# A fused two-model block on one core: output weights converted outside the attention heads, scaled blocks of four norms written to PSUM

## The reference, cut to what matters

```python
a = rmsnorm(h, norm_mix_pre[i])
m = mla_mixer(a, ...) if i % N_MIXERS == 0 else pool_mixer(a, ...)
h = h + rmsnorm(m, norm_mix_post[i])
f = conv_ffn(rmsnorm(h, norm_ffn_pre[i]), ...)
h = h + rmsnorm(f, norm_ffn_post[i])
```

## Time and profile before

| | |
|---|---|
| median of three runs | 1041.41 us (1040.64 to 1042.99) |
| profiled execution | 1039.17 us, span 1037.4 us |
| PE busy | 953.3 us, 92% of the span |
| DVE / ACT / POOL busy | 747.4 / 503.1 / 355.8 us |
| mean granted TensorE clock | 0.933 of full speed |

### The profile page before, as it was taken

How to read it: one execution, slowest core, us unless ns; L and a number is a source line. 1 busy time by engine, 2 the same in 40 slices (tenths; PEclk the granted TensorE clock), 3 DMA queues, 4 the chain that set the end, 5 groups by cost and what they waited for, 6 DMA issues and landing times.

```text
span 1037.4 us, 20011 instructions
## 1 busy us (share of the span) xinstructions
PE 953.3 (92%) x7208; PEld 905.5 (87%) x7208; DVE 747.4 (72%) x1304; ACT 503.1 (48%) x831; POOL 355.8 (34%) x226
## 2 busy tenths in 40 slices
PE   6788999799999899679999989799998999999995
PEld 6786668699999899669999989798998999999995
DVE  7658652689999722658999963477968788786566
ACT  5464333555555443455556643345345545454432
POOL 4421003422222454342222246532125433335543
PEclk9898558799999999789999999989999999999998
DMA  7223001334444445113445545415323555565531
GB/s 268 103 82 122 1 0 42 122 123 162 162 162 177 168 173 206 41 41 123 162 167 178 198 164 202 169 67 196 121 82 133 174 191 202 170 225 175 200 122 41
DMA packets 20848, 145.64 MB, mean 140 GB/s; under 512 B 2480, under 2 KB 4032, under 8 KB 5440
## 3 DMA queue, kind: packets, MB, share of 16 engines
q1 hardware_dynamic: 20800, 144.99, 39.3%
HBM read 143.94 MB, written 1.05 MB: 140 GB/s over the span
## 4 chain that ended last, share of the span: by engine, by line
PE 32%; DVE 10%; ACT 5%; issue 5%; ACTq 1%; DVEq 0%; POOL 0%; POOLq 0%
PE bank L380 10%; PE bank L382 9%; PE bank L381 9%; DVE conv_out L1231 3%; ACT w_high L776 3%; DVE w_low L1108 2%; ACT conv_out L845 1%; ACT w_high L773 1%; PE bank L664 1%; DVE conv_out L1473 1%; DVE gla_q_level L1432 0%; PE bank L444 0%; PE bank L692 0%; DVE conv_out L1580 0%; DVE gla_s_diag L1454 0%
## 5 line engine op out<-in xcount | busy, mean ns | idle before, releaser
L380 PE MATMUL bank<-u_high,w_high 128*128 128x256 f32 (+2 forms) x1472 | 432.8, 294 | 32.2 <-DVE u_low L1117 19.5
L1600 POOL TENSOR_TENSOR w_low<-raw,w_high 128x512 fp32r<-128x512 f32 (+1 forms) x121 | 278.9, 2305 | 510.8 <-ACT w_high L776 510.8
L381 PE MATMUL bank<-u_low,w_high 128*128 128x256 f32 (+2 forms) x1472 | 424.6, 288 | 0.0
L382 PE MATMUL bank<-u_high,w_low 128*128 128x256 f32 (+2 forms) x1472 | 423.6, 288 | 0.0
L380 PEld LDWEIGHTS bank<-u_high,w_high 128*128 128x128 f32 x1472 | 285.0, 194 | 44.6 <-issue 22.8
L1108 DVE TENSOR_TENSOR w_low<-raw,w_high 128x768 fp32r<-128x768 f32 (+4 forms) x120 | 214.8, 1790 | 139.9 <-ACT w_high L776 138.6
L381 PEld LDWEIGHTS bank<-u_low,w_high 128*128 128x128 f32 x1472 | 285.1, 194 | 0.0
L382 PEld LDWEIGHTS bank<-u_high,w_low 128*128 128x128 f32 x1472 | 284.5, 193 | 0.0
L776 ACT ACTIVATE w_high<-raw 128x1280 fp32r<-128x1280 f32 (+4 forms) x120 | 206.6, 1721 | 69.6 <-PE bank L382 64.0
L380 PE MATMUL bank<-x_high,w_high 128*128 128x256 f32 (+1 forms) x608 | 172.8, 284 | 11.0 <-DVE x_low L1208 4.7
L382 PE MATMUL bank<-x_high,w_low 128*128 128x256 f32 (+1 forms) x608 | 172.5, 284 | 0.0
(11 more groups left out here) (180 smaller groups left out, 946.0 us busy)
## 6 DMA issues: line engine op xcount, KB each, us to landing
raw<-w_up_dram SPq DMA_DIRECT2D x66, 1024.0 KB, 4.8
raw<-w_down_dram SPq DMA_DIRECT2D x24, 1408.0 KB, 6.1
raw<-w_gin_c_dram SPq DMA_DIRECT2D x4, 1536.0 KB, 6.5
raw<-w_wo_dram SPq DMA_DIRECT2D x4, 1024.0 KB, 4.7
raw<-w_wout_dram SPq DMA_DIRECT2D x4, 1024.0 KB, 4.8
raw<-w_pgate_dram SPq DMA_DIRECT2D x4, 1024.0 KB, 4.8
raw<-w_gin_v_dram SPq DMA_DIRECT2D x2, 1024.0 KB, 4.9
raw<-w_gin_g_dram SPq DMA_DIRECT2D x2, 1024.0 KB, 5.4
```

Source lines behind the costliest of these rows:

```text
L380: nc.tensor.matmul(out, hi, rhi, start=start, stop=False)
L381: nc.tensor.matmul(out, hi, rlo, start=False, stop=False)
L382: return nc.tensor.matmul(out, lo, rhi, start=False, stop=stop)
L1600: nc.gpsimd.tensor_tensor(wl[n % 2][:, at], raw[n % 2][:, at], wh[n % 2][:, at].bitcast(F32), ALU.subtract).then_inc(low_parts_g, 1)
```

## The change

It has four edits. (1) The first output unit's high part is made before the loop over the heads, the second's at s = 16. (2) Of the first output unit DVE converts 128 of 2048 columns, at s = 16, and POOL the other 1920; the second unit's DVE part comes at s = 18. (3) In `add_post` the scaled block goes to PSUM, alternately to columns 64 and up of bank 6 and to a bank that the next unit doesn't use, and the add reads it from there. (4) POOL waits for the norm's "inverse" before its `low` of the unit that follows the last chunk, in all four norms.

```diff
 def vector_cols(n):
+    if n == FIRST_UNIT["wo"]:
+        return P
     return UNITS[n]["tiles"] * P // 3 if UNITS[n]["name"] == "uqn" else (3 * UNITS[n]["tiles"] // 4) * P
# ScalarE
             heads_out("uk", K)
+            high(FIRST_UNIT["wo"])
             for s in range(NH + 4):
-                if s in (2, 3):
-                    high(FIRST_UNIT["wo"] + s - 2)
+                if s == NH:
+                    high(FIRST_UNIT["wo"] + 1)
# VectorE, add_post
+                spare = 3 * (unit % 2) + 2
+                normed = bank[NORM_BANK][:, 64:64 + Tm], bank[spare][:, 0:Tm]
                 def scale(c):
-                    nc.vector.tensor_tensor(m[:, c, 0:Tm], m[:, c, 0:Tm], bank[R_BANK][:, 0:Tm], ALU.mult)\
+                    nc.vector.tensor_tensor(normed[c % 2], m[:, c, 0:Tm], bank[R_BANK][:, 0:Tm], ALU.mult)\
                         .then_inc(*S.step(f"{name} normed {c}"))
...
-                        nc.vector.tensor_tensor(h[:, c, T1 - Tm:T1], h[:, c, T1 - Tm:T1], m[:, c, 0:Tm], ALU.add)\
+                        nc.vector.tensor_tensor(h[:, c, T1 - Tm:T1], h[:, c, T1 - Tm:T1], normed[c % 2], ALU.add)\
# VectorE, heads
-                if s in (3, 4):
-                    low(FIRST_UNIT["wo"] + s - 3)
+                if s in (NH, NH + 2):
+                    low(FIRST_UNIT["wo"] + (s - NH) // 2)
# GpSimd: fpost0 and fpost1 (in down), post0, post1
+                    else:
+                        pool.wait_ge(*done(f"{name} inverse"))
                     low(n0 + c + 2)
...
+                if u == 3:
+                    pool.wait_ge(*done("post0 inverse"))
                 low(FIRST_UNIT["wo"] + u + 2)
...
+            pool.wait_ge(*done("post1 inverse"))
             low(FIRST_UNIT["pool"] + 2)
```

## The result

| | median, us | runs |
|---|---|---|
| before | 1041.03 | 1040.47 to 1042.99, four runs |
| changed | 1015.59 | 1015.27 to 1016.09, four runs |

The ratio is 0.9753, 95% interval 0.9736 to 0.9770: 25.4 us less. I had said 1037.0, range 1029 to 1042.5. Later runs of the same kernel, in the experiments, showed a second value, so the two groups are given apart: of 17 runs in all, 12 lie between 1014.5 and 1016.5 us, with a mean granted clock of 0.953 to 0.959, and 5 between 1034.4 and 1037.3, with 0.925 to 0.930.

The account below looks back on a forecast made before the run. PE, busy 92%, was taken to bound the kernel through its waits and half-speed clock. 1039.2 (profiled execution) - 7.6 (norms) + 3.2 (heads) = 1034.8; the median 2.2 above gives 1037.0, range 1029 to 1042.5.

Parts of the forecast that it names:

- If the fall comes as long behind it, at 93.5: Early heads: PE's clock falls as long behind the new idle time, ended at 91.9, as before (1.6 us).
- the term of +3.2 us: Heads: later first transposes and the clock's fall put the fourth transposes at 105.2 instead of 101.91; 3.2 us lost.
- rival B: Heads: the clock doesn't fall at all, DVE sets 3.1 us a head, 23 us gained, total 1011; chance 0.13.
- Norms: Four norms: each chain 2.0 us earlier, 8.0 in all, of which 7.6 us taken; bounds 4 to 10.
- DVE first behind the inverse: Norms: DVE's subtraction starts before POOL's and keeps its 1.75 us; POOL finishes about 1.1 us behind.
- adds at 0.43: Norm chunks: two stretched adds per norm fall to 0.43 us; the chain's end moves by 1.0 us.
- scales unchanged: Norm chunks: 32 scales keep their length with PSUM blocks; 0 taken, bounds -0.01 to +0.07 us each.
- C: Norms: POOL wins the race behind the inverse, 1.1 us lost in each, total 1041.4; chance 0.11.
- D: Norms' chunk chain: PSUM operands slow 64 scales and adds; at 0.12 us each, total 1044.7; chance 0.09.
- the waits: Norms: with POOL waiting for the inverse, the stretch of small instructions goes, 4.0 us together.
- POOL's subtraction: Before the heads: POOL's 1920 columns take 4.28 us, from 80.3 to 84.6.
- The stall: Before the heads: DVE's negated maximum waits on POOL, values' copy 3.2 us later, PE idle 2 us before first transposes.

Follow-up runs that it names:

- norms_only: The changed kernel with the output-weight conversions back inside the heads with the usual split, only the norms' edits kept: 1033.2 us, ratio 0.9926.
- after_again: The changed kernel unaltered, run again: 1014.9, 1015.8, 1016.5 us, and 1034.4, 1034.8, 1034.8, 1037.3 us.
- heads_only: The changed kernel with the four norms as before, only the moved output-weight conversions kept: 1019.3, 1019.7, 1022.6 us, and 1041.3, 1041.5 us.
- one_low_early: usual_split with VectorE's 1.75 us subtraction of the first output unit back at s = 3: 1030.8, 1033.4, 1034.5, 1034.5 us, and once 1015.9.
- longer_idle: The changed kernel with three unused VectorE memsets (0.95 us together) ahead of the copy of the last block of values: 1038.2 us, ratio 0.9983.
- no_wait: usual_split without GpSimd's waits for the norms' inverse, scaled blocks still in PSUM: 1014.6 us.
- usual_split: The changed kernel with the first output unit split as all others, VectorE 1536 columns at s = 16, GpSimd 512 before the heads: 1012.1 us, ratio 0.9723.
- pieces: The changed kernel with GpSimd's subtraction of 1920 columns cut into four instructions of 480: 1012.4 us, ratio 0.9736.

## Why the prediction was wrong

**The step that failed** is "If the fall comes as long behind it, at 93.5", on which the term of +3.2 us was built. I had the clock fall in the heads in every case but rival B, to which I gave 0.13 and which lay outside the range; but it is a thing that comes out differently from one execution to the next. In 12 of 17 executions the clock didn't fall behind the new idle time, and then, with VectorE's subtractions gone, no second idle time of that length follows until the last heads. In place of 3.2 us lost, the heads gave 18.1 us (25.4 less the 7.3 of norms_only). All four runs of the result were of this kind; by 12 of 17 that happens in one of four cases, and a slower run among them would have shown a value near the forecast. From the trace of before I had one fall, behind 1.73 us of idle time at 93.8, and one idle time without one, of 0.96. The new idle of about 2 us was longer than both, which speaks for a fall, but two cases do not carry odds of 0.87 to 0.13. With B at 0.3 or more, the range had to reach to it.

**Where it falls, the forecast is near.** In after_again the slower runs are 1034.4 to 1037.3 us beside 1039.7 before, 4.9 us less at their median; the forecast was 4.4 less. The fourth transposes, counted from the first scores, come 2.4 us later than before in after_again and 3.0 in heads_only; I had said 3.3. In the total the loss was 2.4 us (7.3 less 4.9) and, in heads_only, 0.9, against 3.2. The fall came 1.3 and 2.0 us behind the idle time; I had said 1.6. That this time is fixed is not shown: it was 0.6 us in one_low_early, and in longer_idle the clock fell before the idle time ended.

**The terms.** *Norms:* 7.6 us forecast, 7.3 measured in norms_only. DVE first behind the inverse, adds at 0.43, scales unchanged: each as stated; C and D are out. Of the 4.0 us for the waits 2.6 showed in no_wait. *POOL's subtraction:* 4.28 us forecast, 4.31 measured. *The stall:* DVE 3.2 us later forecast, 3.1 measured (3.30 against 0.17); idle 2 us forecast, 1.60 measured, and this 0.4 us may count, as the share of falls changes from 5 of 17 to 12 of 12 between 1.6 and 2.4 us. *Rival B's price:* I had 1011, measured 1015.6: 23 us in the heads forecast, 18.1 measured. Up to the fourth transposes 1.4 us were gained (100.52 against 101.91), where I had counted 2 for what comes before and after the twelve heads. The next ten heads took 3.20 us each where they had taken 4.89, 17.0 us in all; I had counted twelve at 1.8. The last two gained nothing, since the clock goes down at the end of the heads after all, at about 135.8, with PE idle for 1.97 us ahead of it:

```profile
135.13 1.36 PE L550 MATMUL bank<-probs_t,v_tokens 96*64 96x272 f32 x6 [1.97 <-DVE row_inv L1373]
...
140.09 1.12 PE L566 MATMUL bank<-ident,probs 96*96 96x96 f32 x6
```

```profile
134.00:136.00 2.00, 0.87 (x4) 0.66 (x5) 1.93 (x10) 1.38 (x7) 0.00 (x0) 0.95 0.00 0
136.00:138.00 2.00, 1.54 (x9) 1.07 (x7) 0.49 (x4) 2.00 (x3) 0.21 (x1) 0.50 0.34 86
```

The transposes of the last head stand at 140.09 against 158.21, 18.1 us.

**Port and PSUM.** The Trainium skill ("SBUF — State Buffer", section "Who interferes with whom") spoke against edit 2, and usual_split and pieces show that this has a price, about 3 us. Work with a single source in SBUF it counts only where the instruction uses both ports, a condition that the prediction left out; the TENSOR_SCALAR of 96x3 was held up here (3.30 us). The pieces also show that the port pair is given back between GpSimd's instructions, as the rule's "whole instruction" implies. The 62 cycles more that the Trainium skill ("VectorE: DVE Perf Modes", section on the TRN2 errata) gives a PSUM source did not show: the median add went from 0.430 to 0.424 us.

**What stays open** is why one idle time of 1.6 us ends in a fall in one execution and not in another; nothing that the program does differs between them up to there. The traces show such differences elsewhere too: ahead of the heads, where the program is the same, the clock goes down at about 34.0 us in the profile of norms_only (mean 0.76 over 33 to 35) and at about 40.2 in that of the changed kernel (0.80 over 39 to 41).

## What to carry to other kernels

A stretch of light matmul work that runs at full clock is worth guarding: look at every idle time of PE ahead of it, ask which engine caused it, and move that work away. Filling the time may do as well, by ten clean runs. Where a result hangs on such a clock, take many runs and look at them one by one; four equal runs, as here, can hide a second outcome that comes in three of ten. Between VectorE and GpSimd, cut a long GpSimd instruction into pieces, place it behind VectorE's own long one, and give VectorE's waiting chain an operand from PSUM.

## What was not expected of the hardware

The heads at half clock keep PE busy without a gap (4.89 of 4.89 us) for some 50 us, and the clock does not rise; at full clock the same work, with PE busy 2.65 of 3.60 us in the head shown, keeps it up to the last heads. The two levels thus both last, with 3.2 and 4.89 us a head, and in the changed kernel it is decided behind one idle time of 1.6 us at the start which of them it is: 19 us of 1015.
